# Sigmoid of the branch gates split between ScalarE and VectorE, in an encoder trunk on one core

## The chip, the core and the metric

One core of a Trainium2 chip runs the whole program. The metric is the device time in microseconds of one execution. TensorE (PE) does the matmuls, ScalarE (ACT) and VectorE (DVE) work on tiles in SBUF and in PSUM, GpSimd (POOL) and SyncE (SP) issue DMAs here and hardly compute. The engines run their own instruction streams strictly in program order and meet at semaphores.

## The reference

Two layers over 768 tokens (a prompt of 256 and a sample of 512). A layer is a token mixer and a SwiGLU block. The mixer projects the normed input to everything at once, runs three mixers (A: dilated window attention, B: mLSTM, C: differential attention) and merges their outputs under three sigmoid gates per channel:

```
proj = rms_norm(x) @ w_in                      # q/k/v of A, B, C and gate_pre, (768, 3 * 1024)
gates = sigmoid(gate_pre).reshape(B, S, 3, D)
y_a, y_b, y_c = o_a @ w_branch[A], o_b @ w_branch[B], o_c @ w_branch[C]
x = x + (gates[:, :, 0] * y_a + gates[:, :, 1] * y_b + gates[:, :, 2] * y_c) @ w_out
hg, hu = split(rms_norm(x) @ w_ffn_in)
x = x + (silu(hg) * hu) @ w_ffn_out
```

All is float32. This document is about the line `gates = sigmoid(gate_pre)`.

## The kernel before

**Precision.** Every float32 product is made of three matmuls of parts: a high and a low half of each operand (`xh`, `xl`, `wh`, `wl`), where ACT makes the high half of a weight tile by a copy (`split`, L1133, executed at L1139) and DVE the low half by a subtraction (`split`, L1424, executed at L1428).

**One list for all engines.** `schedule()` writes a list `STEPS`, and each engine runs through it in order and does its part of each step. Dense steps (`piece`, `bc`, `gate`, `branch`, `wout`) are projections on TensorE that fill one PSUM bank of three in rotation. Side steps (`a_...`, `b_...`, `c_...`) are the attention and mLSTM work of mixers A, B and C; they are strewn between the dense steps by rules with gaps in units of dense time, so that TensorE has dense work while ACT and DVE prepare the next side step. Since an engine never passes a step of its list, what stands ahead on DVE delays all DVE work behind it.

**A gate step** `("gate", b, d, q)` makes 128 channels (d of 8) of branch b for one half q of the tokens: 24 matmuls into a bank of 128x384. There are 48 per layer. ACT then makes the sigmoid in three activations over a slot of `stage` (`sigmoid`, L1146 to L1150): e = exp(-x) out of PSUM, l = ln(e + 1), exp(-l). The third one raises `act_staged`. TensorE waits for that semaphore (the list `FREED`) before it fills the same bank again, three dense steps later, and POOL waits for it before it stores the slot to `gate_t` in DRAM (`store_staged`, L842). `stage` has three slots; ACT waits for the store of three staged steps before (`stage_slot`). DVE has nothing to do in a gate step, except the low half of a weight tile that stands behind every second one. The gates come back from DRAM when the `branch` steps multiply them with the branch outputs on DVE (L1500).

**Where the 48 gates stand**, in the order of `STEPS`:

- First stretch: the 16 gates of branch 0, beside the merges of mixer A: gate, gate, `turn` (a transpose of the merged output of mixer A), `a_merge` of a later tile, and so on. The last four surround `b_rows`, `b_gates` (gate preparation of mixer B), and behind them stand the four `b_scan` steps and `b_columns`.
- Mixer B: most of the 32 gates of branches 1 and 2. One unit u is: gate (called A below), `b_qk` u, `b_norm` u-1, `b_decay` u, `b_conv` u+1, gate (B, with a weight tile), `b_score` u, `b_silu` u+1, gate (C), gate (D, with a weight tile), `b_out` u. On TensorE `b_out` waits for the score products of DVE (L1666, L1667, semaphore `b_wt`), `b_qk` for the DVE work behind the previous `b_out` (L1680 to L1690, `b_h`), `b_score` for ACT's copies. ACT's part of `b_decay` waits for the sums of DVE (L1655), its part of `b_out` are squares and a small reciprocal square root (L1301, L1143, L1144), for which the DVE part of `b_norm` (L1697) waits.
- Mixer C: the last ten gates, one per slot. A slot is: gate, `c_mix` u-1 (L1731 to L1734 on DVE), `c_score` u (scores on TensorE, L2050; maximum on DVE, L1723; two exponentials on ACT, L1331), `c_turn` u-2, `c_out` u-3, now and then a `c_fold`, `c_norm` or `c_scale`.

Both `Exp` and `Ln` lie in the one activation table that is loaded ahead of the list (L1131).

Of the kernel before, what the change touches and what calls it, by code (L numbers as in the profile page):

```python
# [21 lines left out]
ALU = mybir.AluOpType  # L22
ACT = mybir.ActivationFunctionType
# [315 lines left out]
def schedule():  # L339
# [74 lines left out]

HEADS = {s: i for i, s in enumerate([s for s in STAGED if s[0] == "piece" and (
    s[1] % 3 < 2 if s[1] < 9 else s[1] in (C_C, C_C + 1))])}
PLAIN = {s: i for i, s in enumerate([s for s in STAGED if s not in HEADS])}


# [33 lines left out]
def build(nc, io):  # L453
    ctx = ExitStack()
    with ctx:
# [126 lines left out]
        w_lo = sem("w_lo")  # L582
        d_done = sem("d_done")
        act_staged = sem("act_staged")
        mixed = sem("mixed")
        stored = [sem(f"stored{i}") for i in range(SLOTS)]
        mix_stored = [sem(f"mix_stored{i}") for i in range(GSLOTS)]
# [110 lines left out]
        def ps_bank(n):  # L698

            return ps[:, n % BANKS, :]  # L700
# [26 lines left out]
        with nc.Fori(0, DEPTH) as layer:  # L727
            with nc.Block() as block:
# [105 lines left out]
                def _(pool):  # L834
# [7 lines left out]
                    def store_staged(step):  # L842
                        m = STAGE[step]
                        slot = stage[:, m % SLOTS, :]
                        if step in HEADS:
                            pool.wait_ge(h_ready, HEADS[step] + 1)
                        else:
                            pool.wait_ge(act_staged, PLAIN[step] + 1)
                        if step[0] == "bg":
                            dst, src = gates_b[:, HALVES[step[1]]], slot[0:16, 0:HALF_TOK]  # L850
                        elif step[0] == "gate":
                            _, b, d, q = step
                            dst, src = gate_t[b, d * P:(d + 1) * P, HALVES[q]], slot[:, 0:HALF_TOK]
                        elif step[0] == "bc":
                            _, h, q = step
                            dst, src = conv_in[h * P:(h + 1) * P, HALVES[q]], slot[:, 0:HALF_TOK]
                        else:
                            c, t = step[1:]
                            rows = slice(t * P, (t + 1) * P)
                            if c < 9:  # L860
                                dst, src = qkv_a[rows, c % 3, c // 3, :], slot[:, 0:A_W]
                            elif c < C_C:
                                dst = b_vo[rows, c - C_BVO].rearrange("p h e -> p (h e)")
                                src = slot[:, 0:B_W]
                            else:
                                dst, src = qkv_c[rows, c - C_C, :], slot[:, 0:C_W]
                        pool.dma_start(dst, src).then_inc(stored[m % SLOTS], 16)  # L867
                        if m == len(STAGED) - 1:
                            wait_stage(m)
                            for i in range(GSLOTS - 2):  # L870
                                load_gate(i)
# [257 lines left out]
                def _(act):  # L1129
# [51 lines left out]
                    def dense(step):  # L1181
# [15 lines left out]
                        elif kind == "bc":  # L1197
                            dst = stage_slot(step)[:, 0:HALF_TOK]
                            act.wait_ge(d_done, n + 1)
                            act.activation(dst, ps_bank(n)[:, 0:HALF_TOK], ACT.Copy).then_inc(act_staged, 1)  # L1200
                        elif kind == "bg":
                            dst = stage_slot(step)[0:16, 0:HALF_TOK]
                            act.wait_ge(d_done, n + 1)
                            act.activation(dst, ps_bank(n)[0:16, 0:HALF_TOK], ACT.Copy).then_inc(act_staged, 1)
                        elif kind == "gate":
                            dst = stage_slot(step)[:, 0:HALF_TOK]
                            act.wait_ge(d_done, n + 1)
                            sigmoid(dst, ps_bank(n)[:, 0:HALF_TOK]).then_inc(act_staged, 1)
                        elif kind == "branch" and step[1] == 2:
                            i = MIXES[step]  # L1210
                            act.wait_ge(mixed, i + 1)
                            act.activation(mix_rows(True, step[2])[:, HALVES[step[3]]], gated[i % GSLOTS], ACT.Copy
                                           ).then_inc(r_hi, 1)
                        elif kind == "turn":
                            _, b, t = step
                            k = MIX_ROWS[b][1]
                            act.wait_ge(d_done, n + 1)
                            act.activation((xh if b == 1 else oh)[:, 0:k, t * P:(t + 1) * P],
                                           ps_bank(n)[:, 0:k * P].rearrange("p (k n) -> p k n", k=k),
                                           ACT.Copy).then_inc(t_hi, 1)  # L1220
# [199 lines left out]
                def _(dve):  # L1420
# [69 lines left out]
                    def dense(step):  # L1490
                        n = INDEX[step]
                        kind = step[0]
                        if step in HEADS:
                            normed_heads(step, ps_bank(n))
                        elif kind == "branch":
                            i = MIXES[step]
                            e = gated[i % GSLOTS]
# [689 lines left out]
```

## Time and profile before

| | us |
|---|---|
| median of three runs | 3354.35 |
| lowest and highest | 3353.36, 3357.91 |
| the profiled execution's own time | 3353.53 |
| its span, from first to last instruction | 3351.9 |
| TensorE busy in it | 3170.0 |
| DVE, ACT busy | 1541.5, 1186.5 |

The mean granted clock of TensorE over the span is 0.982 of full speed. The rows further down are of four kinds. The page's part 1 gives busy time per engine. A window row gives a stretch of the span, its length and, engine by engine (PE, PEld, DVE, ACT, POOL), the busy us and the number of instructions, then the granted clock, the DMA share and GB/s. A group row gives a source line, engine, operation, the tiles written and read, shapes and count, then busy us and mean ns of one, then the idle time just ahead of them. A timeline row gives the start in us from the span's start, the duration and the instruction; in square brackets stands how long the engine was idle before it and who ended that. The stretches are those of layer 1; layer 2 repeats them about 1666 us later.

### The profile page before, as it was taken

How to read it: one execution, taken by the hardware profiler on the slowest of the kernel's cores; microseconds unless marked ns; L12 is line 12 of the kernel's file. 1: busy time of each engine (PE TensorE's matmuls, PEld its weight loads, DVE VectorE, ACT ScalarE, POOL GpSimd, SP SyncE). 2: the span in 40 equal slices, each digit the busy share in tenths (PEclk: the TensorE clock that was granted, in tenths of full speed). 3: DMA queues.
4: the chain of work that ended last, by engine and by line, in shares of the span. 5: the costliest groups of instructions: out<-in, count | busy, mean ns of one | idle time of the engine just before them, and what ended most of it. 6: DMA issues, size and time to landing. Idle time of an engine off the chain costs nothing. (4 is left out here: it accounts for less than half of the span.)

```text
span 3351.9 us, 46018 instructions
## 1 busy us (share of the span) xinstructions
PE 3170.0 (95%) x17652; PEld 2906.0 (87%) x17652; DVE 1541.5 (46%) x3149; ACT 1186.5 (35%) x2656; POOL 509.5 (15%) x879
## 2 busy tenths in 40 slices
PE   6899999899989999999978999998999999999998
PEld 6899989688878999999878999887887889999997
DVE  5445226644465343443463452365444653434433
ACT  3234434356543211211143344343665422211210
POOL 0111321222242000000001114212222410000000
PEclk9999999999999999999989999999999999999999
DMA  4334444343375122211033344434433742212211
GB/s 162 108 105 123 135 126 129 124 132 120 111 192 181 56 60 61 75 60 52 32 131 104 107 129 134 134 112 124 144 119 122 183 157 63 72 41 75 75 45 62
DMA packets 273323, 358.65 MB, mean 107 GB/s; under 512 B 27377, under 2 KB 209841, under 8 KB 273129
## 3 DMA queue, kind: packets, MB, share of 16 engines
q1 hardware_dynamic: 213576, 179.41, 18.0%
q0 software_dynamic: 59552, 176.68, 16.9%
q8 instruction: 118, 1.93, 0.2%
q14 instruction: 77, 0.62, 0.1%
HBM read 264.42 MB, written 91.59 MB: 106 GB/s over the span
## 5 line engine op out<-in xcount | busy, mean ns | idle before, releaser
L1833 PE MATMUL ps<-wh,xh 128*128 128x384 f32 (+1 forms) x1440 | 537.1, 373 | 18.6 <-DVE wl L1428 11.9
L1835 PE MATMUL ps<-wh,xl 128*128 128x384 f32 (+1 forms) x1440 | 521.2, 362 | 0.0
L1834 PE MATMUL ps<-wl,xh 128*128 128x384 f32 (+1 forms) x1440 | 521.1, 362 | 0.0
L1833 PE MATMUL ps<-xh,wh 128*128 128x384 f32 (+1 forms) x1312 | 459.0, 350 | 12.3 <-issue 7.1
L1428 DVE TENSOR_TENSOR wl<-wraw,wh 128x1024 fp32r<-128x1024 f32 (+2 forms) x210 | 232.5, 1112 | 460.5 <-ACT wh L1139 460.2
L1835 PE MATMUL ps<-xh,wl 128*128 128x384 f32 (+1 forms) x1312 | 443.3, 338 | 0.0
L1834 PE MATMUL ps<-xl,wh 128*128 128x384 f32 (+1 forms) x1312 | 443.0, 338 | 0.0
L1907 PE MATMUL ps<-xl,wh 128*128 128x384 f32 x1280 | 325.0, 334 | 0.0
L1907 PE MATMUL ps<-xh,wl 128*128 128x384 f32 x1280 | 324.9, 334 | 0.0
L1907 PE MATMUL ps<-xh,wh 128*128 128x384 f32 x1280 | 324.7, 334 | 0.0
L1833 PEld LDWEIGHTS ps<-wh,xh 128*128 128x128 f32 x1440 | 277.0, 192 | 51.1 <-DVE wl L1428 13.3
L1835 PEld LDWEIGHTS ps<-wh,xl 128*128 128x128 f32 x1440 | 275.7, 191 | 24.1
L1834 PEld LDWEIGHTS ps<-wl,xh 128*128 128x128 f32 x1440 | 276.8, 192 | 22.1
L1793 DVE SCALAR_TENSOR_TENSOR arena<-arena,ps 128x768 f32<-128x768 f32 x44 | 42.0, 954 | 546.1 <-ACT arena L1390 546.1
L1833 PEld LDWEIGHTS ps<-xh,wh 128*128 128x128 f32 (+1 forms) x1312 | 246.5, 188 | 22.5 <-issue 12.3
L1834 PEld LDWEIGHTS ps<-xl,wh 128*128 128x128 f32 (+1 forms) x1312 | 246.7, 188 | 6.3 <-issue 3.8
L1835 PEld LDWEIGHTS ps<-xh,wl 128*128 128x128 f32 (+1 forms) x1312 | 246.4, 188 | 2.5
L1835 PE MATMUL ps<-wh,ol 128*128 128x512 f32 x624 | 243.2, 390 | 0.0
L1834 PE MATMUL ps<-wl,oh 128*128 128x512 f32 x624 | 243.1, 390 | 0.0
L1833 PE MATMUL ps<-wh,oh 128*128 128x512 f32 x624 | 242.7, 389 | 0.0
L867 POOL DMA_DIRECT2D qkv_a<-stage x108 | 59.0, 546 | 1195.1 <-DVE stage L1481 1051.1
L1390 ACT ACTIVATE arena<-ps 128x768 f32<-128x768 f32 x44 | 35.8, 815 | 560.0 <-PE ps L1907 534.3
(229 smaller groups left out, 5207.4 us busy)
## 6 DMA issues: line engine op xcount, KB each, us to landing
wraw<-in_w_in SPq DMA_DIRECT2D x96, 512.0 KB, 3.8
wraw<-in_w_ffn_in SPq DMA_DIRECT2D x88, 512.0 KB, 4.0
wraw<-in_w_in SPq DMA_DIRECT2D x72, 384.0 KB, 3.6
wraw<-in_w_ffn_out SPq DMA_DIRECT2D x44, 512.0 KB, 3.3
qkv_a<-stage POOLq DMA_DIRECT2D x108, 192.0 KB, 2.2
gate_t<-stage POOLq DMA_DIRECT2D x96, 192.0 KB, 2.2
stage<-gate_t POOLq DMA_DIRECT2D x78, 192.0 KB, 4.3
mix_t<-stage POOLq DMA_DIRECT2D x52, 192.0 KB, 3.8
```

Source lines behind the costliest of these rows:

```text
L867: pool.dma_start(dst, src).then_inc(stored[m % SLOTS], 16)
L1390: act.activation(f_e[:, ft, :].rearrange("p (h n) -> p h n", h=2), ps[:, bank:bank + 2, 0:HALF_TOK], ACT.Tanh, scale=0.5).then_inc(f_ex, 1)
L1428: dve.tensor_tensor(wl[:, half, j, 0:w], wraw[:, n % RAW, 0:w], wh[:, half, j, 0:w].bitcast(F32), ALU.subtract).then_inc(w_lo, 1)
L1793: fch.link(dve.scalar_tensor_tensor(e2, e2, 1.0, ps[:, bank:bank + 2, 0:HALF_TOK], ALU.add, ALU.mult))
L1833: pe.matmul(out, ah, bh, start=first, stop=False)
L1834: pe.matmul(out, ah, bl, start=False, stop=False)
L1835: return pe.matmul(out, al, bh, start=False, stop=last)
L1907: mm = pe.matmul(pair[0:cols, q, 0:HALF_TOK], w[:, half, j, sl_], v[:, k, q * HALF_TOK:(q + 1) * HALF_TOK], start=(k == 0 and w is wh and ...
```

## The change

The three activations of a gate become one activation, exp(-x) out of PSUM, which raises `act_staged` itself. DVE waits for it, adds one to the slot, and takes the reciprocal in place; that raises a new semaphore `gate_ready`, for which the store on POOL waits. `act_staged` still frees the PSUM bank, now behind the first activation. Other uses of `sigmoid` in mixer B stay as they are. Nothing changes on TensorE.

```
+GATES = {s: i for i, s in enumerate([s for s in STAGED if s[0] == "gate"])}
...
+        gate_ready = sem("gate_ready")
...
                         if step in HEADS:
                             pool.wait_ge(h_ready, HEADS[step] + 1)
+                        elif step in GATES:
+                            pool.wait_ge(gate_ready, GATES[step] + 1)
                         else:
                             pool.wait_ge(act_staged, PLAIN[step] + 1)
...
                             act.wait_ge(d_done, n + 1)
-                            sigmoid(dst, ps_bank(n)[:, 0:HALF_TOK]).then_inc(act_staged, 1)
+                            act.activation(dst, ps_bank(n)[:, 0:HALF_TOK], ACT.Exp, scale=-1.0).then_inc(act_staged, 1)
...
                         if step in HEADS:
                             normed_heads(step, ps_bank(n))
+                        elif kind == "gate":
+                            g = stage[:, STAGE[step] % SLOTS, 0:HALF_TOK]
+                            dve.wait_ge(act_staged, PLAIN[step] + 1)
+                            chain.link(dve.tensor_scalar(g, g, 1.0, None, ALU.add))
+                            dve.reciprocal(g, g).then_inc(gate_ready, 1)
```

What this does to the order on the engines, at the places that matter. VectorE in the first stretch, from the end of one merge (L1583) to the start of the next (L1567, afterwards L1592 and L1576), before:

```order
L1583 TENSOR_TENSOR arena<-arena 128x384 [waits dve_chain]
L1428 TENSOR_TENSOR wl<-wraw,wh 128x1024 [waits w_hi]
L1517 TENSOR_TENSOR ol<-ps,oh 128x3x128 [waits t_hi]
L1567 TENSOR_TENSOR arena<-arena 128x6 [waits d_done,m_loaded0]
L1568 TENSOR_TENSOR arena<-arena 128x6 [waits dve_chain]
```

and in the changed kernel:

```order
L1592 TENSOR_TENSOR arena<-arena 128x384 [waits dve_chain]
L1502 TENSOR_SCALAR stage<-stage 128x384 [waits act_staged]
L1503 RECIPROCAL stage<-stage 128x384 [waits dve_chain]
L1432 TENSOR_TENSOR wl<-wraw,wh 128x1024 [waits w_hi]
L1502 TENSOR_SCALAR stage<-stage 128x384 [waits act_staged]
L1503 RECIPROCAL stage<-stage 128x384 [waits dve_chain]
L1526 TENSOR_TENSOR ol<-ps,oh 128x3x128 [waits t_hi]
L1576 TENSOR_TENSOR arena<-arena 128x6 [waits d_done,m_loaded0]
```

Two pairs of gate work stand between the merges, the first ahead of the weight tile and the second ahead of the transpose's low half.

VectorE in mixer B, from the last score product through silu to the work behind `b_out`, before:

```order
L1667 TENSOR_TENSOR arena<-ps,arena 128x512
L1644 TENSOR_TENSOR arena<-arena 128x512 [waits b_exp]
L1428 TENSOR_TENSOR wl<-wraw,wh 128x1024 [waits w_hi]
L1680 COPY unit_s<-ps 128x8 [waits b_store,b_nd]
L1681 SCALAR_TENSOR_TENSOR unit_s<-unit_s 128x8 [waits dve_chain]
```

and in the changed kernel, up to the start of `b_norm` (L1706, L1697 before):

```order
L1676 TENSOR_TENSOR arena<-ps,arena 128x512
L1653 TENSOR_TENSOR arena<-arena 128x512 [waits b_exp]
L1502 TENSOR_SCALAR stage<-stage 128x384 [waits act_staged]
L1503 RECIPROCAL stage<-stage 128x384 [waits dve_chain]
L1502 TENSOR_SCALAR stage<-stage 128x384 [waits act_staged]
L1503 RECIPROCAL stage<-stage 128x384 [waits dve_chain]
L1432 TENSOR_TENSOR wl<-wraw,wh 128x1024 [waits w_hi]
L1689 COPY unit_s<-ps 128x8 [waits b_store,b_nd]
...
L1699 TENSOR_TENSOR arena<-arena 128x512 [waits dve_chain]
L1502 TENSOR_SCALAR stage<-stage 128x384 [waits act_staged]
L1503 RECIPROCAL stage<-stage 128x384 [waits dve_chain]
L1706 TENSOR_TENSOR arena<-arena,unit_s 128x512 [waits b_rs]
```

Gates C and D stand ahead of the work behind `b_out`, gate A between that work and `b_norm`; gate B stands in the same way between `b_conv` and the score products.

## Rows read from the trace of the kernel before

**Rows 1.** The page, part 1: busy us (share of the span) and instructions.
```profile
PE 3170.0 (95%) x17652; PEld 2906.0 (87%) x17652; DVE 1541.5 (46%) x3149; ACT 1186.5 (35%) x2656; POOL 509.5 (15%) x879
```

**Rows 2.** Windows by stage: stretch, length, each engine's busy us, PE clock, DMA.
```profile
495.00:568.00 73.00, 69.19 (x390) 67.82 (x389) 42.74 (x100) 38.37 (x70) 12.83 (x24) 0.98 0.42 135
767.50:794.50 27.00, 26.54 (x148) 23.35 (x148) 14.71 (x35) 18.92 (x47) 4.49 (x8) 1.00 0.33 99
836.77:898.68 61.91, 60.51 (x351) 50.95 (x348) 26.86 (x43) 36.36 (x89) 10.56 (x17) 1.00 0.26 85
```

**Rows 3.** Groups by line, shapes apart: busy us, mean ns | idle before.
```profile
L1149 ACT ACTIVATE stage<-stage 128x384 f32<-128x384 f32 x96 | 50.4, 525 | 3.0
L1150 ACT ACTIVATE stage<-stage 128x384 f32<-128x384 f32 x96 | 50.4, 525 | 3.0
...
L1744 DVE RECIPROCAL unit_s<-c_z 128x2 f32<-128x2 f32 x8 | 1.3, 157 | 0.0
L1744 DVE RECIPROCAL unit_s<-c_z 128x4 f32<-128x4 f32 x8 | 1.4, 169 | 0.0
L1684 DVE RECIPROCAL unit_s<-unit_s 128x4 f32<-128x4 f32 x8 | 1.4, 178 | 0.3
L1684 DVE RECIPROCAL unit_s<-unit_s 128x8 f32<-128x8 f32 x8 | 1.6, 203 | 0.3
...
L1617 DVE TENSOR_SCALAR arena<-arena 4x256 f32<-4x256 f32 x4 | 1.1, 282 | 0.1
L1617 DVE TENSOR_SCALAR arena<-arena 4x512 f32<-4x512 f32 x4 | 1.7, 414 | 0.1
...
L1582 DVE TENSOR_TENSOR arena<-arena 128x384 f32<-128x384 f32 x12 | 6.7, 558 | 0.4
```

**Rows 4.** Waits of TensorE: line, awaited, us in total, times, longest.
```profile
PE ps L1833 <- ACT stage L1150: 3.2, 2, 1.6
```

**Rows 5.** Timeline of VectorE, first stretch: start us, us, instruction [idle before <-releaser].
```profile
515.32 0.15 DVE L1567 TENSOR_TENSOR arena<-arena 128x6 f32<-128x6 f32 x1
...
519.91 1.23 DVE L1428 TENSOR_TENSOR wl<-wraw,wh 128x1024 fp32r<-128x1024 f32 x1
523.50 0.56 DVE L1517 TENSOR_TENSOR ol<-ps,oh 128x384 fp32r<-128x384 f32 x1 [2.37 <-ACT oh L1218]
```

**Rows 6.** Timeline of TensorE at the transposes of b_columns.
```profile
595.09 2.68 PE L1986 MATMUL ps<-ident,arena 4*128 4x4 f32 x24 [3.54 <-DVE arena L1617]
```

**Rows 7.** Timeline of PE, DVE and ACT, a unit of mixer B.
```profile
767.83 4.73 PE L2024 MATMUL ps<-arena 128*128 128x129 f32 x40 [0.44 <-DVE arena L1667]
...
777.37 0.69 DVE L1697 TENSOR_TENSOR arena<-arena,unit_s 128x512 f32<-128x512 f32 x1 [1.91 <-ACT unit_s L1144]
...
781.18 0.40 ACT L1288 ACTIVATE arena<-arena 128x128 f32<-128x128 f32 x1 [1.37 <-DVE arena L1655]
...
787.78 0.47 ACT L1148 ACTIVATE stage<-ps 128x384 f32<-128x384 f32 x1
...
790.35 1.23 DVE L1428 TENSOR_TENSOR wl<-wraw,wh 128x1024 fp32r<-128x1024 f32 x1 [7.00 <-ACT wh L1139]
...
794.81 4.73 PE L2024 MATMUL ps<-arena 128*128 128x129 f32 x40 [0.44 <-DVE arena L1667]
```

**Rows 8.** Timeline of DVE and ACT, two slots of mixer C.
```profile
871.37 1.22 DVE L1723 TENSOR_REDUCE c_s<-ps 128x2 f32<-128x1024 f32 x1 [3.23 <-PE ps L2050]
...
877.53 0.49 ACT L1148 ACTIVATE stage<-ps 128x384 f32<-128x384 f32 x1 [2.48 <-PE ps L1835]
...
880.78 0.16 DVE L1731 RECIPROCAL c_s<-c_s 128x1 f32<-128x1 f32 x1
...
881.89 1.22 DVE L1723 TENSOR_REDUCE c_s<-ps 128x2 f32<-128x1024 f32 x1
```

**Rows 9.** Windows behind the idle time of rows 6.
```profile
596.00:598.00 2.00, 2.00 (x18) 1.98 (x18) 1.69 (x4) 1.64 (x3) 0.00 (x0) 0.50 0.00 0
602.00:604.00 2.00, 2.00 (x10) 1.61 (x10) 1.93 (x6) 0.04 (x1) 0.44 (x1) 1.00 0.46 176
```

## The prediction

> **What bounds the kernel now.** I read the page's busy times first, then the windows by stage, then the timeline of VectorE (DVE) and ScalarE (ACT) inside each stage with gates. TensorE is busy 3170.0 of 3351.9 us and DVE 1541.5 [rows 1], so over the whole span DVE looks half idle. That average is the trap of this case: the change adds DVE work only in 96 places (48 gate steps in each of two layers), and what counts is the room there. Three stretches of layer 1 hold its 48 gates, and layer 2 repeats them. In the first (16 gates, branch 0, with the merges of mixer A between them) DVE is busy 42.74 of 73 us; in one unit of mixer B with four gates 14.71 of 27.00; in the ten-gate stretch beside mixer C 26.86 of 61.91 [rows 2]. TensorE is above 94% in all three, so it is the bound today, and the forecast rests on whether DVE stays below it.
>
> **What is removed.** Two activations of a 128x384 tile, 525 ns each, per gate [rows 3]: 96 x 1.05 = 101 us of ACT. ACT is busy 18.92 of 27.00 us in a unit of mixer B [rows 2], and TensorE waited for the last of the three activations for 3.2 us in all, twice 1.6 [rows 4]. So the direct gain is at most 3 us, and it lies in the first stretch, which DVE will now hold anyway. I count zero. The PSUM bank is freed 1.05 us sooner, which with three banks in rotation and that 3.2 us as the only wait on it buys nothing more.
>
> **What is added.** Per gate one DVE add of a constant and one reciprocal, both 128x384 in SBUF, the second behind the first by a semaphore. The add: a TENSOR_SCALAR takes 282 ns for 256 and 414 for 512 elements [rows 3], so 348 for 384. The handover from one to the other is 0.4 us over 12 cases where dependent DVE operations follow each other in the merge, 0.03 each [rows 3]. The reciprocal is the open price: no large one exists in this trace. The small ones give a slope. With the same operands, 157 ns for 2 and 169 for 4 elements (6.0 ns each), 178 for 4 and 203 for 8 (6.25 ns each) [rows 3]. A plain TENSOR_TENSOR does 384 elements in 558 ns [rows 3], under 1.5 ns each. From below, a reciprocal like any other pass would cost 0.56 us; by the slope it is 0.178 + 380 x 0.00625 = 2.55 us. From above, the steepest line that the rows allow runs across the two kinds, 157 for 2 to 203 for 8, 7.7 ns an element and 3.10 us. I take the slope within a kind, since it shows in two independent pairs and fixed overhead cannot make it. So one gate costs G = 0.35 + 0.04 + 2.55 = 2.94 us of DVE, 96 of them 282 us.
>
> The Trainium skill (VectorE: DVE Perf Modes, First, the fixed hardware budget) says that the reciprocal is an iterative divide with a repeat count of 8, at a clock of 0.96 GHz (same page, Specifications). Read as eight cycles an element, my estimate from that page is 8.3 ns an element and 3.35 us in all, and by it the forecast below would be 72 us higher; the rows' 6.0 to 6.25 ns speak for less, and no run so far shows a long one. Its page Perfetto Trace Analysis (Optimizing Scalar/DVE Operations) advises moving work from DVE to ScalarE where DVE is saturated, the reverse of this change.
>
> **First stretch.** One period is two gates, a transpose, a merge: merge from 515.32 to 519.91 (4.59), split 1.23, low half of the transpose 0.56, idle 2.37 before it [rows 5]; together 8.7 us, the pace that TensorE sets. With two gates DVE needs 4.59 + 1.23 + 0.56 + 5.88 = 12.3, so it is the bound. For the stretch: 42.74 + 16 x 2.94 = 89.8 busy, and some 6 us of waits that stay (small dependent steps of six merges, the ACT logarithm between the two halves of the gate preparation of mixer B), 96 against 73: **+23**. Behind it stand the scans, for which TensorE waits already (3.54 us [rows 6]), so nothing absorbs it.
>
> **Units of mixer B.** DVE and ACT hand work to and fro in program order. Today, from one b_out on TensorE (767.83) to the next (794.81), 26.98 us pass [rows 7]. In the new order DVE has, behind the score products that start b_out: silu (one pass over 512 elements, some 0.7), gates C and D 5.88, a split 1.23, together 7.8 us, and only then the work after b_out. Row by row on: that work, from the end of b_out at 772.56 to 775.46, 2.9; ACT's squares, 1.9 (the idle time before 777.37); gate A, which must be finished before b_norm, 0.5 exponential + 2.94 = 3.4; b_norm and the decay sums, 777.37 to 781.18, 3.8; ACT's decay exponentials and a sigmoid, 781.18 to 787.78, 6.6; gate B 3.4 (today 2.57 from 787.78 to 790.35); split and score products to the next b_out, 790.35 to 794.81, 4.5 [rows 7]. Sum 34.3, **+7.3** an interval. In the trace TensorE waits 0.44 at this place, so there is no slack. Five intervals lie beside gates: four at +7.3, the first, which is entered with nothing queued and half as long operands, at about a third, 2.4. Together +31.6, and +3 for the one gate that stands ahead of the first c_score.
>
> **Mixer C.** One gate per interval, nine intervals in the 61.91 us. DVE's maximum starts at 871.37; ACT is through its exponentials and copies at 877.53 - 2.48 = 875.05, so 3.7 later [rows 8]. Then the gate's exponential 0.5, G 2.94, and from 880.78 to 881.89 1.1 us of c_mix ahead of the next maximum [rows 8]: 8.2 against 6.9 by TensorE. Some slots lack a copy (0.5), others carry a split or a c_norm; I take 75.5 for the nine, **+13.5**. The last gate's store comes later by about 1.9 (2.94 against 1.05) and its reload gates the first mix: +1.5.
>
> **Clock.** After the idle 3.54 us [rows 6] the granted clock is 0.50 in the rows at 596 to 598 and back at 1.00 at 602 to 604 [rows 9], so half speed for about 6 us. In the B units TensorE will idle 5 to 7 us right ahead of b_out, 4.73 us at full clock [rows 7], twice that at half: it then ends 9.5 us in, later than the 7.8 at which DVE comes free. +1.5 in four intervals, +6. In the other two stretches the waits are short or TensorE is not on the path.
>
> **Sum.** 23 + 31.6 + 3 + 13.5 + 1.5 + 6 = 78.6 a layer, 157 for two. Profiled execution: span 3351.9, its own time 3353.53, which is 0.8 under the median of 3354.35. 3353.5 + 157 = 3510. Each microsecond of reciprocal is worth 16 + 18 + 1 + 9 + 1 = 45 us a layer, 90 in all.
>
> **Rivals.**
> Dear reciprocal: a long one runs at the steepest line, 7.7 ns an element, 3.10 us. 0.55 x 90 = +50: 3560. For it: only up to 8 elements are seen. Against: the two pairs agree and show no rise.
> Cheap reciprocal: per element it costs like other passes and the slope is a start-up effect; G = 0.95. Then the first stretch needs 42.74 + 15.2 + 6 = 64 of 73 us, in a B unit DVE waits for TensorE again, the chain is 4.7 + 2.9 + 1.9 + 1.4 + 3.8 + 6.6 + 1.4 + 4.5 = 27.2 against 26.98, and the 3 us of bank waits go: 3350 to 3360, about 3354, not slower. It decides at about G = 1 in the B units and 1.5 in the first stretch ((73 - 42.74 - 6)/16). Against: the slope.
> Absorbed: the reciprocal costs 2.55 but the gates slip into DVE's idle time in the B and C stretches, because ACT, relieved by 1.05 us a gate, comes earlier than my chain has it; only the first stretch pays in full and the others a third: 23 + 17 a layer, 3433. For it: DVE's load there stays under the time, 14.71 + 11.8 = 26.5 of 27.0 and 26.9 + 29.4 = 56 of 62 [rows 2]. Against: both orders are fixed, and gate A stands ahead of b_norm.
>
> **How the numbers follow.** As forecast 0.70 (its own range 3465 to 3555, from a slope of 6.0 to 6.5 and 30 us for stalls misjudged); dear 0.14; absorbed 0.10; cheap 0.06. The predicted time is 3510. The range 3435 to 3590 leaves out the cheap case and the outer edges of the others. A measurement of this kernel tells 0.2%, 6.7 us, from no change: faster by more 0.02 and within 0.05, both from the cheap case and a little beyond, slower 0.93.
>
> **What would show it.** A row RECIPROCAL stage 128x384 x96 near 2550 ns, and TENSOR_SCALAR near 350. DVE above 90% busy where the merges are, with turns 12 us apart. b_out to b_out about 34 to 36 us, with waits of TensorE on DVE's score products (none above 0.44 now) and a clock of 0.5 behind them. Granted clock over the run below 0.98. If the reciprocal takes 0.6 us, everything above falls; if it takes 2.5 and the time is under 3440, the chain through gate A or C and D is wrong.

## The result, and the profile after

The changed kernel takes 3493.42 us (median of four runs, 3490.92 to 3496.26) where the kernel before took 3356.13 (median of four): a ratio of 1.041, 95% interval 1.0392 to 1.0428. It is slower, by 137 us. The forecast was 3510, with a range of 3435 to 3590. The profiled execution took 3496.26 us with a span of 3494.6.

The page, part 1, against [rows 1]:

```profile
PE 3222.5 (92%) x17652; PEld 2944.4 (84%) x17652; DVE 1803.7 (52%) x3341; ACT 1083.5 (31%) x2464; POOL 509.9 (15%) x879
```

DVE gained 262 us of work, ACT lost 103, and DVE is still only 52% busy, the same trap as before. The three groups of a gate, shapes apart (busy us, mean ns, then the idle time ahead), against [rows 3]:

```profile
L1503 DVE RECIPROCAL stage<-stage 128x384 f32<-128x384 f32 x96 | 245.1, 2553 | 3.3
L1212 ACT ACTIVATE stage<-ps 128x384 f32<-128x384 f32 x96 | 45.8, 482 | 55.3 <-PE ps L1844 49.9 <-DMA gate_t<-stage 5.5
L1502 DVE TENSOR_SCALAR stage<-stage 128x384 f32<-128x384 f32 x96 | 33.6, 350 | 138.9 <-ACT stage L1212 138.9
```

The windows by stage, against [rows 2]: the first stretch, one unit of mixer B, and nine intervals of mixer C.

```profile
495.00:591.00 96.00, 79.73 (x416) 74.75 (x415) 85.97 (x132) 21.36 (x39) 13.05 (x24) 0.95 0.36 114
807.10:840.70 33.60, 29.23 (x149) 26.04 (x149) 25.67 (x43) 14.71 (x38) 4.46 (x7) 0.91 0.27 78
...
892.22:971.29 79.07, 70.69 (x354) 58.20 (x353) 51.23 (x61) 27.49 (x75) 10.55 (x17) 0.89 0.20 66
```

Only the first is a stretch in which DVE is full (85.97 of 96.00 us). In the other two both TensorE and DVE have room, 4 and 8 us, 8 and 28 us: there it is a chain that DVE and ACT walk in turn. DVE in the first stretch, one period from the last step of a merge to the last step of the next, against [rows 5] (the lines left out are the merge itself):

```profile
506.73 0.56 DVE L1592 TENSOR_TENSOR arena<-arena 128x384 f32<-128x384 f32 x1
507.21 0.35 DVE L1502 TENSOR_SCALAR stage<-stage 128x384 f32<-128x384 f32 x1
507.59 2.55 DVE L1503 RECIPROCAL stage<-stage 128x384 f32<-128x384 f32 x1
510.06 1.16 DVE L1432 TENSOR_TENSOR wl<-wraw,wh 128x1024 fp32r<-128x1024 f32 x1
511.14 0.35 DVE L1502 TENSOR_SCALAR stage<-stage 128x384 f32<-128x384 f32 x1
511.52 2.55 DVE L1503 RECIPROCAL stage<-stage 128x384 f32<-128x384 f32 x1
513.99 0.49 DVE L1526 TENSOR_TENSOR ol<-ps,oh 128x384 fp32r<-128x384 f32 x1
...
518.43 0.56 DVE L1592 TENSOR_TENSOR arena<-arena 128x384 f32<-128x384 f32 x1
```

No row shown waits, and in the lines left out DVE waits once, 0.28 us for ACT, as it did before. A period is 518.43 - 506.73 = 11.70 us, and the 2.37 us of idle time of [rows 5] are gone. A unit of mixer B, TensorE's `b_out` and DVE, against [rows 7]:

```profile
807.10 7.42 PE L2033 MATMUL ps<-arena 128*128 128x129 f32 x40 [5.24 <-DVE arena L1676]
...
807.56 0.36 DVE L1502 TENSOR_SCALAR stage<-stage 128x384 f32<-128x384 f32 x1
...
814.55 0.17 DVE L1689 COPY unit_s<-ps 128x8 f32<-128x8 f32 x1 [0.17 <-PE ps L2033]
...
819.71 0.36 DVE L1502 TENSOR_SCALAR stage<-stage 128x384 f32<-128x384 f32 x1 [2.29 <-ACT stage L1212]
820.10 2.55 DVE L1503 RECIPROCAL stage<-stage 128x384 f32<-128x384 f32 x1
822.57 0.63 DVE L1706 TENSOR_TENSOR arena<-arena,unit_s 128x512 f32<-128x512 f32 x1
...
833.42 0.36 DVE L1502 TENSOR_SCALAR stage<-stage 128x384 f32<-128x384 f32 x1 [4.95 <-ACT stage L1212]
...
840.68 1.66 PE L2033 MATMUL ps<-arena 128*128 128x129 f32 x6 [4.37 <-DVE arena L1676]
```

(A row of many instructions at the end of a window, as the last one, counts only those inside it.) The interval is 33.58 us against 26.98. TensorE waits 4 to 5 us ahead of `b_out` where it waited 0.44, and `b_out` itself takes 7.42 us where it took 4.73. Waits of TensorE that grew (us in all, times, longest), against [rows 4]:

```profile
PE ps L2033 <- DVE arena L1676: 26.8, 8, 5.2
PE ps L2009 <- DVE arena L1699: 20.2, 8, 4.0
PE ps L1842 <- DVE wl L1432: 20.1, 9, 4.5
PE ps L2059 <- ACT arena L1335: 17.3, 17, 3.0
...
PE ps L2045 <- DMA arena<-qkv_c: 12.9, 2, 6.8
```

The last one is in no part of the prediction: `c_fold`, the transposes ahead of the last `b_out`, waits for a load of `qkv_c`, 2.0 us in all before. POOL and TensorE there in layer 1, before and then in the changed kernel, and the clock behind the wait:

```profile
816.51 1.49 POOL L1030 DMA_DIRECT2D arena<-qkv_c  x2
822.35 0.66 PE L2036 MATMUL ps<-ident,arena 128*128 128x128 f32 x4 [1.00 <-DMA arena<-qkv_c]
827.45 4.63 PE L2024 MATMUL ps<-arena 128*128 128x129 f32 x40
```

```profile
869.81 0.56 POOL L871 DMA_DIRECT2D gate_t<-stage  x1 [8.75 <-issue]
870.39 1.48 POOL L1034 DMA_DIRECT2D arena<-qkv_c  x2
876.17 1.11 PE L2045 MATMUL ps<-ident,arena 128*128 128x128 f32 x4 [6.01 <-DMA arena<-qkv_c]
883.49 4.63 PE L2033 MATMUL ps<-arena 128*128 128x129 f32 x40
...
876.17:880.90 4.73, 4.73 (x16) 4.73 (x17) 3.18 (x2) 0.60 (x1) 0.71 (x2) 0.50 0.38 111
```

Counted from `b_out` 6 (794.81 and 840.68), the load goes out after 29.7 us instead of 21.7, 8.0 later. Two things hold it: ACT's last decay exponentials (semaphore `b_dec`), which end 6.1 us later by the chain of DVE and ACT, and the store of gate B, which stands ahead of it in POOL's program. That store waits for the reciprocal now and not for ACT's third activation, which is the other 1.9. Behind the wait the granted clock is 0.50, and from the fold to the last `b_out` TensorE takes 7.32 us instead of 5.10.

**Where the time went**, from the starts of TensorE's steps in the two traces (delay of the changed kernel, and its growth over each stretch):

| stretch | forecast, a layer | layer 1 | layer 2 |
|---|---|---|---|
| first stretch (to `b_out` 2) | 23 | 23.1 | 22.9 |
| mixer B (to `c_score` 0) | 31.6 + 3 + 6 = 40.6 | 32.9 | 31.6 |
| mixer C (nine intervals) | 13.5 | 16.3 | 13.7 |
| last gate (next interval) | 1.5 | 1.2 | 0.7 |
| sum | 78.6 | 73.5 | 68.9 |

Together 142.4 of the 142.7 us by which the spans differ.

### The profile page after: what moved, and what is told of

Its sections match the earlier page's. It is cut to its first block, busy times and chain, and to the rows that moved or that the text cites. A ratio compares the mean times of both kernels' runs of the same rounds, so it can differ in the third digit from the quotient of the medians.

```text
span 3494.6 us, 46018 instructions
## 1 busy us (share of the span) xinstructions
PE 3222.5 (92%) x17652; PEld 2944.4 (84%) x17652; DVE 1803.7 (52%) x3341; ACT 1083.5 (31%) x2464; POOL 509.9 (15%) x879
## 4 chain that ended last, share of the span: by engine, by line
PE 32%; DVE 9%; issue 3%; ACT 3%; DMA 2%; POOL 1%; SPq 0%; ACTq 0%; POOLq 0%; DVEq 0%
PE ps L1916 10%; PE ps L1842 6%; PE ps L1843 6%; PE ps L1844 6%; DVE stage L1503 2%; DVE wl L1432 1%; PE ps L1985 1%; PE ps L1970 0%; PE ps L1959 0%; PE ps L1947 0%; DMA wraw<-in_w_in 0%; PE ps L2059 0%; DVE stage L1502 0%; DVE stage L1476 0%; DVE stage L1473 0%
## 5 line engine op out<-in xcount | busy, mean ns | idle before, releaser
L1842 PE MATMUL ps<-xh,wh 128*128 128x384 f32 (+1 forms) x1312 | 466.0, 355 | 15.3 <-issue 7.1
L1503 DVE RECIPROCAL stage<-stage 128x384 f32<-128x384 f32 x96 | 245.1, 2553 | 3.3
```

The source lines that it names most:

```text
L1503: dve.reciprocal(g, g).then_inc(gate_ready, 1)
L1842: pe.matmul(out, ah, bh, start=first, stop=False)
```

## Experiments

### Is it the length of the reciprocal?

```
                             chain.link(dve.tensor_scalar(g, g, 1.0, None, ALU.add))
-                            dve.reciprocal(g, g).then_inc(gate_ready, 1)
+                            dve.tensor_scalar(g, g, 0.5, None, ALU.mult).then_inc(gate_ready, 1)
```

> The changed kernel with its reciprocal replaced by a multiplication of the same tile by 0.5 (so the gates are not sigmoids; a row TENSOR_SCALAR of 0.35 us stands where the reciprocal of 2.55 us stood). All waits, semaphores and the place in VectorE's order stay. Theory (it is the length of the reciprocal): back to the time of before within 5 us, 3350 to 3362, b_out to b_out near 27 us. Rival (it is VectorE as a link in the order, whatever it does): most of the 137 us stay, above 3420.

Measured: 3346.68 us (ten runs, 3340.29 to 3354.11) against 3357.84, ratio 0.9971 (0.9961 to 0.9981). With the same order, the same semaphores and a step of 0.36 us in place of 2.55, all of the loss is gone, and 11 us more. So it is the length, not the handover or the second semaphore, and what the rest of the change brings is more than the 3 us that the prediction granted and the zero that it counted.

Then only 128 of the 384 columns:

```
-                            dve.reciprocal(g, g).then_inc(gate_ready, 1)
+                            dve.reciprocal(g[:, 0:128], g[:, 0:128]).then_inc(gate_ready, 1)
```

> The changed kernel with the reciprocal over 128 of 384 columns only (the other columns keep 1 + exp(-x)); by the slope 0.95 us. It puts a gate at G = 1.35 us, near the points at which the prediction said that VectorE decides (1.5 in the first stretch, about 1 in the B units). Theory: first stretch nearly unchanged, +0.8 in a B interval, C unchanged; 3364, at most 3372. Rival (loss in proportion to the reciprocal's time without a threshold): 3356 + 137 x 1.35 / 2.94 = 3419.

Measured: 3366.73 us (seven runs), ratio 1.003 (1.0019 to 1.0042). Its group row:

```profile
L1503 DVE RECIPROCAL stage<-stage 128x128 f32<-128x128 f32 x96 | 91.5, 953 | 3.3
```

953 ns for 128 and 2553 for 384 elements are 6.25 ns an element with 153 ns ahead of them. G is 0.35 + 0.04 + 0.95 = 1.34 here, and it costs 20 us over the multiply version (whose G is about 0.75), where the full one costs 147. The price is not proportional: 34 us for each us of G between 0.75 and 1.34, then (3493 - 3367) / 1.60 = 79. And twice the reciprocal:

```
+                            chain.link(dve.reciprocal(g, g))
                             dve.reciprocal(g, g).then_inc(gate_ready, 1)
```

> The reciprocal is taken twice in a row at every gate (the second undoes the first, so the stored value is 1 + exp(-x) and not the gate): its 2.55 us once more. Theory: VectorE's chain is the bound wherever gates lie, so each further us costs the 90 us that the prediction worked out, or more, since the slack of the first 1 to 1.5 us is spent already: 2.55 + 0.03 of handover by 90 is 232, about 3725, 3700 to 3740. Rival: the work still slips into idle time in part (64 and 79 us of the 172 and 79 us stretches show VectorE idle by a quarter and a third) and it is 3600 to 3650. In the units of mixer B the interval goes from 33.6 to 33.6 + 4 x 2.58 = 43.9 by the prediction's chain through A and B and C and D, and to 38.8 if only the two gates ahead of b_norm count.

Measured: 3725.68 us (four runs, 3724.86 to 3727.71), ratio 1.1102 (1.1085 to 1.1119). That is 232 us more for 2.58 us more, 90 us for each, the slope of the prediction; nothing of the second reciprocal slips into idle time. From one `b_out` to the next (these two rows are TensorE's in the timeline) there are 43.66 us, where four more reciprocals in the chain, 33.58 + 4 x 2.58, give 43.9:

```profile
832.06 6.29 PE L2034 MATMUL ps<-arena 128*128 128x129 f32 x40 [7.59 <-DVE arena L1677]
...
875.72 4.51 PE L2034 MATMUL ps<-arena 128*128 128x129 f32 x21 [8.00 <-DVE arena L1677]
```

### The change in the first stretch alone

`GATES` holds the gates of branch 0 only; the others keep the three activations on ACT.

```
-GATES = {s: i for i, s in enumerate([s for s in STAGED if s[0] == "gate"])}
+GATES = {s: i for i, s in enumerate([s for s in STAGED if s[0] == "gate" and s[1] == 0])}
```

> The change only for the 16 gates of branch 0 in each layer, the first stretch; the other 32 keep three activations. Theory (the first stretch loses 23 us a layer and nothing behind it gives any back): 3356 + 46 = 3402. Rival (slack behind the scans absorbs part): under 3385.

Measured: 3398.87 us in a single run, 41 over the median of before; the spans of the two profiled executions differ by 45.3. `b_columns` starts at 617.62 instead of 595.09, +22.5, and by the tenth `c_score` of the layer the delay is 24.7. The first stretch is a term of its own, and in this trace nothing behind it takes it back.

### Is it where the work stands, or how much it is?

The add and the reciprocal of a gate one dense step later on DVE, so that DVE never stands at a gate that ACT has just begun:

```
+                    def flush():
+                        while late:
+                            step = late.pop()
+                            ...
+                            dve.reciprocal(g, g).then_inc(gate_ready, 1)
                     def dense(step):
+                        flush()
...
-                            dve.reciprocal(g, g).then_inc(gate_ready, 1)
+                            late.append(step)
```

> The changed kernel, but VectorE does the add and reciprocal of a gate one dense step later, ahead of its own work of the next dense step, so that c_mix, b_norm, the score products and the work behind b_out stand ahead of the gate that they stood behind. Same work, same load. Theory (the loss in mixers B and C is the order, gates in the chain between VectorE, ScalarE and TensorE): first stretch +20 instead of 23, B units 29.4 instead of 33.6 us, C near the pace of before; 3432 in all. Rival (it is VectorE's load, the order does not matter): within 10 us of the changed kernel, 3493.

Measured: 3463.64 us (four runs), ratio 1.0323 (1.0305 to 1.034): 30 us better than the change, 30 worse than the theory. The trace shows both halves. Three intervals of mixer B take 27.1, 27.8 and 29.1 us, where they took 24.0, 27.0 and 27.0 before and 31.1, 33.3 and 33.6 with the change; DVE is busy 21.9 to 25.5 us in them. But TensorE now waits 39.1 us in four waits for `qkv_c`. TensorE at `c_fold`, and POOL ahead of it:

```profile
892.13 1.11 PE L2053 MATMUL ps<-ident,arena 128*128 128x128 f32 x4 [11.10 <-DMA arena<-qkv_c]
```

```profile
885.92 0.54 POOL L871 DMA_DIRECT2D gate_t<-stage  x1 [20.58 <-DVE stage L1502]
886.45 1.51 POOL L1034 DMA_DIRECT2D arena<-qkv_c  x2
```

POOL stands 20.58 us at a store that waits for a reciprocal which is now due one dense step later, and the load that TensorE needs is the next in its queue. To test this, the store was held back too, until the next staged tile's store or mix:

```
+                    held = []
...
                         if step in STAGE:
+                            release()
+                            if step in GATES and STAGE[step] != len(STAGED) - 1:
+                                held.append(step)
+                            else:
+                                store_staged(step)
-                            store_staged(step)
```

> The version with the gate's add and reciprocal one dense step later, and in addition each gate's store held back on the POOL queue until the next staged tile's store or mix, so that the loads of qkv_c behind it no longer stand behind its wait. Theory (the queue took the place of the wait): the 39.1 us that TensorE waited for qkv_c in four waits go back to the 2.0 of rows of before, and the time falls from 3464 to 3427 or so, 3420 to 3440; what is left over the kernel before is the first stretch (+43) and some 30 us where VectorE is simply full. Rival: behind the loads VectorE stands at its own limit (in those stretches it is busy 26.3 of 27.0 us), its waits take over, and no more than 10 us come back, 3454 or more.

Measured: 3424.03 us (four runs, 3423.00 to 3425.64), ratio 1.0198 (1.0182 to 1.0214), and no wait for `qkv_c` is left in its list of waits. The theory held: of the 137 us, 30 went with the place on DVE and 40 more with the place on POOL, work unchanged. The rest, 67 us, is the first stretch (`b_columns` at 617.02, +21.9 in layer 1) and small ones in B and C (in layer 1 the delay grows by 5 us between `b_out` 2 and 7 and by 4 over the nine intervals of C). Another 7 us a layer come behind the eleventh `c_score`, where the changed kernel loses 0.7 in layer 1; they were not taken apart.

### What does the clock cost?

Spare matmuls into the bank that is filled next, ahead of six waits of a layer, so that TensorE isn't idle there:

```
+                    dummies = {("b_out", 5): 22, ("b_out", 6): 22, ("c_score", 1): 14, ("c_score", 3): 9,
+                               ("c_score", 7): 8, ("c_score", 8): 10}
+                    def fill(step):
+                        n = 1 + max(INDEX[s] for s in STEPS[:STEPS.index(step)] if s in INDEX)
+                        wait_bank(n)
+                        for _ in range(dummies[step]):
+                            pe.matmul(ps_bank(n)[:, 0:HALF_TOK], xh[:, 0, 0:P], xh[:, 0, HALVES[0]], start=True, stop=True)
```

> The changed kernel with 8 to 22 spare matmuls ahead of six waits of each layer (b_out 5 and 6, c_score 1, 3, 7, 8), into the bank that TensorE fills next, so that it does not idle there and its clock stays at full. They fit into the idle time; nothing else moves. Theory (VectorE's chain alone sets the pace, the clock only stretches work that has slack): no change in the units of mixer B, interval 33.6 as now, and in all 3493, within 5. Rival (the clock is a cause of its own): b_out after the waits takes 4.7 and not 7.4 us, the three places of mixer C where VectorE waits for a gate that TensorE made slowly lose 3 to 5 us together, and the time falls by 6 to 14 to about 3483. Third: the spare matmuls delay TensorE where the wait is shorter than in the profile, and it is 5 to 10 us slower.

Measured: 3485.53 us (four runs), ratio 1.039 (1.0375 to 1.0406). TensorE at `b_out` 5:

```profile
796.94 3.98 PE L1941 MATMUL ps<-xh 128*128 128x384 f32 x22
802.35 4.73 PE L2044 MATMUL ps<-arena 128*128 128x129 f32 x40 [1.43 <-DVE arena L1676]
```

`b_out` is back at 4.73 us, and the intervals from `b_out` 4 to 5 and from 5 to 6 are 33.31 and 33.32, against 33.32 and 33.58: at most 0.3 us. The interval of the ratio overlaps that of the change, so the part in mixer C was run beside the changed kernel in one session:

> The changed kernel itself once more, unaltered, so that the version with spare matmuls in mixer C alone is set against it in the same session; 3491 to 3496.

> The changed kernel with spare matmuls ahead of the four waits of mixer C alone (c_score 1, 3, 7, 8), none ahead of b_out 5 and 6. Theory, from the trace of the version that had both: in mixer C the low clock costs 3.4 us a layer and in the units of mixer B 0.3, so this one gains nearly all that the other did: interval of b_out 33.6 as in the changed kernel, nine intervals of c_score 75.7 instead of 79.1, and 6 to 8 us under the changed kernel of the same session, 3486. Rival: the gain of the version with both came from somewhere else or from the spread between sessions, and this one is within 2 us of the changed kernel.

Measured: 3496.23 us for the changed kernel (five runs, 3492.01 to 3497.35), ratio 1.042 (1.0406 to 1.0435), and 3487.40 with the spare matmuls in C alone (five runs, 3486.52 to 3492.23), ratio 1.04 (1.0386 to 1.0415). The medians are 9 us apart, the ranges just touch and the intervals overlap, so the size rests on the traces. The window of the nine intervals, to be set against 79.07 us at a clock of 0.89:

```profile
889.40:965.15 75.75, 71.65 (x395) 59.83 (x394) 51.50 (x62) 27.38 (x75) 10.58 (x17) 1.00 0.21 69
```

That is 3.3 us less, and in layer 2 of this pair 75.75 against 79.16; together 6.7. The intervals of mixer B, without spare matmuls, are 33.30 and 33.45 here, so what is saved does not lie there. The trace of the changed kernel shows how C loses. Two windows of it, DVE's next gate, and then the same gate with the spare matmuls:

```profile
902.00:908.00 6.00, 6.00 (x18) 4.50 (x17) 5.04 (x6) 0.78 (x3) 2.04 (x3) 0.50 0.34 122
908.00:914.00 6.00, 6.00 (x33) 4.99 (x33) 2.73 (x2) 2.88 (x7) 0.00 (x0) 0.98 0.27 83
```

```profile
911.23 0.36 DVE L1502 TENSOR_SCALAR stage<-stage 128x384 f32<-128x384 f32 x1 [3.55 <-ACT stage L1212]
```

```profile
907.25 0.36 DVE L1502 TENSOR_SCALAR stage<-stage 128x384 f32<-128x384 f32 x1 [2.38 <-ACT stage L1212]
```

After a wait of 3.00 us the granted clock is 0.50, the lower of the two levels, for about 6 us; the next gate's matmuls fall into it, so ACT gets the gate late, and DVE, whose chain with ACT sets the pace here, stands 3.55 us instead of 2.38 (4.49 at the next place). In layer 2 of the first profiled execution the second place lost nothing (7.53 us from one `c_score` to the next instead of 10.37), and there C costs 13.7 instead of 16.3 us.

### What does the relief of ScalarE bring?

First the bank alone: three activations on ACT as before, but the first frees the bank and the third raises `gate_ready`; DVE gets nothing.

```
                             act.activation(dst, ps_bank(n)[:, 0:HALF_TOK], ACT.Exp, scale=-1.0).then_inc(act_staged, 1)
+                            act.wait_ge(act_staged, PLAIN[step] + 1)
+                            chain.link(act.activation(dst, dst, ACT.Ln, bias=1.0))
+                            act.activation(dst, dst, ACT.Exp, scale=-1.0).then_inc(gate_ready, 1)
```

> The gate stays on ScalarE as in the kernel before (exponential, logarithm, exponential), but with the change's second semaphore: the first activation alone reads PSUM and raises the first semaphore, so TensorE's bank is free about 1.05 us sooner, and only the store waits for the third. VectorE gets nothing. This is one part of the change alone. Theory (release): of the 11 us that the kernel with a multiply in place of the reciprocal gained, the wait of TensorE on the third activation (3.2 us in all, rows 4) is part; about 3353, 2 to 4 us under the kernel before, ratio 0.9990. Rival (relief): the 11 us come from the two activations that ScalarE no longer runs, which this kernel still runs, and it gives no change, ratio 1.000. If the release carries all of it, ratio 0.997.

Measured: 3350.23 us (eleven runs) against 3356.61, ratio 0.9987 (0.9977 to 0.9996). A gain of 0.1%, hardly beyond what can be measured. Then the exponential alone, with no add and no reciprocal anywhere (both DVE lines deleted, POOL waits for `act_staged`):

> The add and the reciprocal are left out, so the stored gate is exp(-x) alone, and the store waits for the exponential: ScalarE has one activation a gate, VectorE nothing. It bounds what the ScalarE side of the change can bring with no price on VectorE. Theory: VectorE's two cheap passes of 350 ns in the multiply version cost nothing, since it has room below about 1 us a gate; so the same as that version, 3346, 3340 to 3352. Rival: those 0.7 us still stood in a chain 45 times a layer at part of their length, and without them it is 3325 or less.

Measured: 3335.36 us (four runs), ratio 0.9937 (0.9922 to 0.9952). Neither the theory nor the rival: 21 us under before, 11 under the multiply version. So two activations of ACT less are worth 15 us on top of the early release, 21 with it, and the two cheap DVE steps of the multiply version already give half of that back. The interval of `b_out` is 26.29 with TensorE never waiting, against 26.98. The chain is in [rows 7]: until 790.35 DVE waits 7.00 us for a weight's high half, and ACT makes that behind the gate's three activations, the first of which starts at 787.78. In the waits of TensorE this shows as 0.44 us on DVE, never as ACT. By the starts of the steps, 4.1 us a layer of the gain lie in mixer B and 2.1 in the nine intervals of C.

From this, a mixed version: early release everywhere, and DVE takes the reciprocal at four gates a layer, behind the next silu.

```
+LATE = {("gate", 1, d, 0): i for i, d in enumerate((1, 3, 5, 7))}
...
+                            if step not in LATE:
                                 act.wait_ge(act_staged, PLAIN[step] + 1)
...
+                        while late:
+                            s = late.pop()
+                            ...
+                            dve.reciprocal(g, g).then_inc(late_ready, 1)
```

> The version whose gates stay on ScalarE with the first activation alone freeing the bank, except four gates a layer (the first half of directions 1, 3, 5 and 7 of branch 1, each of them the gate ahead of a weight split that VectorE sits idle for, 7.0 us in rows 7): those have the exponential alone on ScalarE and the add and reciprocal on VectorE, after the next silu, where VectorE was idle for 1.69 us and then 1.31, with a semaphore of their own. Theory (ScalarE's 1.05 us at that place stand in the chain to b_out, VectorE's 2.94 fall into idle time): the interval from b_out to b_out goes from 26.98 to 26.3, as in the version with the exponential alone, 0.7 in four intervals of two layers is 5 to 6 us, and the time is 3344, ratio 0.9970 to the kernel before. Rival: 2.94 against 3.0 of room is no room, the handling of b_out comes later and the intervals stay at 27 or grow, 3350 to 3358.

Measured: 3350.64 us (ten runs, 3345.21 to 3352.91) against 3356.69, ratio 0.9978 (0.9968 to 0.9987). The mechanism is there: DVE takes the gate where it stood idle, and the interval between the two `b_out` is 26.29.

```profile
767.73 0.36 DVE L1509 TENSOR_SCALAR stage<-stage 128x384 f32<-128x384 f32 x1
768.12 2.55 DVE L1510 RECIPROCAL stage<-stage 128x384 f32<-128x384 f32 x1
770.62 1.23 DVE L1440 TENSOR_TENSOR wl<-wraw,wh 128x1024 fp32r<-128x1024 f32 x1
772.44 0.17 DVE L1702 COPY unit_s<-ps 128x8 f32<-128x8 f32 x1 [0.59 <-PE ps L2046]
```

```profile
767.77 4.63 PE L2046 MATMUL ps<-arena 128*128 128x129 f32 x40
...
794.06 1.17 PE L2046 MATMUL ps<-arena 128*128 128x129 f32 x9
```

But only two of the four intervals shorten (by 0.7 each): the other two, 23.86 and 32.73, stay at 23.96 and 32.64, so it is 3 us and not 5 to 6. It is faster than both kernels, if only by 0.2% than the one before, but the intervals of its ratio and of that of early release alone overlap; whether the four gates add anything isn't settled.

## The prediction, point by point

**The bound.** Right: the loss lies in the three stretches with gates and nowhere else, 142.4 of 142.7 us.

**What is removed: counted at zero.** Wrong, in size and in reason. It was read off the list of waits (3.2 us for the third activation), and there the bank wait is indeed worth 3 us or little more (early release: 0.13%). But ACT's time also stands in the chain that leads to a wait on DVE, which that list shows under DVE. The exponential alone shows 21 us. It shows in the cheap rival, put at 3354, where the multiply version took 3347; the main forecast it hardly touches, since its chains in B and C count ACT's part of a gate at the new 0.5 us anyway.

**What is added.** The slope read from two pairs of small reciprocals, 6.0 and 6.25 ns an element over a factor of 48 to 96 in length, gave 2.55 us; measured 2553 ns. The add was 348 and is 350. The Trainium skill (VectorE: DVE Perf Modes, First, the fixed hardware budget) has a repeat count of 8 for the reciprocal; read as eight cycles an element at its 0.96 GHz that was an estimate of 3.35 us, and the trace doesn't agree: 6.25 ns are six such cycles. The dear rival (3.10) and the cheap one (0.56) fell with the same row.

**First stretch: +23.** Measured 23.1 and 22.9. The period is 11.70, not 12.3, since each step starts a little before the profile has the one ahead of it end: a gate advances the chain by 2.85 us, the split by 1.08, the low half by 0.42, the merge by 4.50. The 96 us of the stretch came out, but by two errors of 4 us that cancel: DVE is busy 85.97 of them, not 89.8, and idle 10.0, not 6.

**Units of mixer B: +7.3 an interval.** Measured +7.1, +6.3, +6.6 and, in the last, +10.2. The chain through gate A and gate B is right row by row: 34.3 forecast, 33.6 found; doubling the reciprocal adds 10.1 where four times 2.58 is 10.3. The entry interval was put at 2.4 and is 2.7. The 3 us for the gate ahead of the first `c_score` are not found: from the last `b_out` to it, 8.73 us in both traces. The last interval was the omission. Its length is set by the load of `qkv_c`, 8.0 us later than before (7.5 in layer 2), and by the low clock behind the wait for it, 2.2 us (1.3). Most of the 8.0 is the chain that the prediction knew; the 1.9 us that the new semaphore adds at the head of POOL's queue, and that anything stands behind that store at all, it never asked for. TensorE's wait grows by 5.0 and 5.9 us in the two layers, but that is not the price of the queue: in layer 1 TensorE reaches the fold 2.9 us later itself, as its `b_out` ran at the low clock. The changed kernel was not run with the load moved ahead of the store; in the version with deferred gates, holding the store back took all of the wait away.

**Mixer C: +13.5.** The prediction put the nine intervals at 75.5 us. With the clock held up they take 75.75, against 62.78 before (+13.0; the window of [rows 2] is 0.9 us short of them, hence the prediction's +13.5). In the profiled execution of the changed kernel it is +16.3 in layer 1 and +13.7 in layer 2.

**Clock: +6 in B, nothing elsewhere.** This step failed: the prediction had the places wrong. In B the low clock does lengthen `b_out`, from 4.73 to 7.42 us, but DVE is busy with gates C and D and a split for 7 us in that time and then waits for `b_out` for 0.17; the estimate doubled the whole 4.73, and the trace has the low clock only for the first 5 to 6 us of the step. Holding the clock up there changed at most 0.3 us. What B does lose to the clock is behind the wait for `qkv_c`, 2.2 and 1.3 us, where TensorE goes to the last `b_out` without another wait; this is read from the two traces, no run holds the clock up there. In C, where it said that waits are short, they were up to 3.00 us, and the low clock behind them costs 3.3 where it shows. The forecast had 12 us for both layers, in four intervals of B; the traces have 3.5 in one place of B and 4.0 to 6.7 in C. The total of the step is near, by luck.

**The rivals.** Absorbed (3433) needed the gates to slip into idle time. At 3493 it is 60 us off; the intervals of B grew by 6.3 us and more, where a third would be 2.4, and the second reciprocal of the doubled version costs 90 us for each us. The thresholds of the cheap rival, G = 1 in B and 1.5 in the first stretch, hold up as the places where the price gets steep: at G = 1.34 the loss is 20 us of 147. Below them a step is not free, though: leaving out the last 0.75 us gained another 11 us. The page of the Trainium skill that advises moving work from a saturated VectorE to ScalarE (Perfetto Trace Analysis, Optimizing Scalar/DVE Operations) fits the first stretch, where work moved the other way filled DVE, 86 of 96 us, and cost 23; in B and C DVE never was saturated, and they lost all the same.

**The sum.** 157.2 was forecast and 142.4 is in the traces: mixer B 16.7 too high, mixer C 3.0 too low, the last gate 1.1 too high. The 16.7 are the clock term (12) and the gate ahead of `c_score` (6), neither found where it was put, less 1.3 by which the intervals together came out longer: six of them 4.0 us in all under 7.3 each, the last one of each layer 4.7 in all over it (3.5 of that is clock), the entries 0.6 over 2.4 each. So part of the closeness is luck: the terms missed by more than the sum. The medians differ by 137, the two profiled executions by 143, since one lies 2.8 us above its median and the other 2.6 below.

## What to carry over

Before work moves to an engine that looks half idle, look at the stretches where the work lies, and write down the chain that the engines walk in turn: the price of a step is what it adds to that chain, and a list of waits names only the last link of it. Then ask of each new semaphore which queue stands at it and what lies behind in that queue: here a store that no engine was waiting for stood ahead of a load that TensorE needed, and in the version with deferred gates TensorE waited for it up to 11 us. And where the price of an operation is unknown, its slope between two small sizes can be a better guide than its class, as it was here.

## What the runs showed of the hardware

- A reciprocal on VectorE costs 6.25 ns an element over its 153 ns from 4 to 384 elements (178, 203, 953 and 2553 ns for 4, 8, 128 and 384), where an add of a constant takes 350 ns for 384. That makes the reciprocal alone dearer than the two activations that add and reciprocal replace (1.05 us) by 1.5 us.
- Behind a wait of TensorE of 3.00 us its granted clock was 0.50, the 1.2 GHz level, for about 6 us. It costs only where the work in that stretch is on the path: at most 0.3 us an interval beside 7 us of VectorE work, 3.3 us in nine intervals where VectorE waited for a product made in it, 2.2 us where TensorE went on to the next chained step without another wait (5.10 us of work in 7.32). Spare matmuls ahead of the waits kept it at 1.00.
